# A two-block transformer on one core: GpSimd's splitting of weights by stage, the row mask on ScalarE, a restarted bank counter, and one attention branch walked backwards

## The reference

```
for l in range(2):                                  # first block
    h = rmsnorm(x) @ w_in[l]                        # 21 column groups of 128
    o = concat(sparse_attention, gated_linear_attention, spatial_gating)
    x = x + o @ w_out[l]
    h = rmsnorm(x);  x = x + (silu(h @ w_gate[l]) * (h @ w_up[l])) @ w_down[l]
x = rmsnorm(x)
h = rms_norm(x) * (1 + scl) + shift                 # second block
xa, za, q, k, v, zb, ga, gb = split(h @ w_in_2)
y_a = (lru_forward(conv(xa)) + lru_backward(conv(xa))) * silu(za) @ w_pa
y_b = neighbourhood_attention(q, k, v) * silu(zb) @ w_pb
out = rms_norm(x + gate * ((sigmoid(ga) * y_a + sigmoid(gb) * y_b) @ w_o))
```

## Time and profile before

| | us |
|---|---|
| median of 3 runs | 2053.39 |
| lowest and highest run | 2050.51 and 2055.06 |
| the profiled execution, whole | 2054.61 |
| its span, first to last instruction | 2052.6 |
| TensorE busy | 1924.2 (94%) |
| GpSimd busy | 1419.6 (69%) |
| VectorE busy | 1160.2 (57%) |
| ScalarE busy | 615.6 (30%) |
| mean granted clock of TensorE | 0.969 of full speed |

### The profile page before, as it was taken

One profiled execution on the slowest core, in us unless ns is written; L12 is line 12 of the kernel. 1 busy time (PEld: TensorE's weight loads), 2 busy tenths in 40 slices (PEclk: granted clock), 3 DMA queues, 4 the chain that ended last, 5 costly groups with the idle time before them and its releaser, 6 DMA issues.

```text
span 2052.6 us, 28491 instructions
## 1 busy us (share of the span) xinstructions
PE 1924.2 (94%) x10022; PEld 1489.2 (73%) x10022; DVE 1160.2 (57%) x1670; ACT 615.6 (30%) x1116; POOL 1419.6 (69%) x1208
## 2 busy tenths in 40 slices
PE   7898889999999999988899999997999999989997
PEld 5676557888888877755588888885777777768775
DVE  5765774466257347478556704654937666650353
ACT  4124662210011131266531100113036566540111
POOL 8554117988789985511298978886897878757772
PEclk9999989999999999999999999998999999999998
DMA  5132002343334222300124433542132233222221
GB/s 204 53 96 80 22 11 83 122 143 108 97 121 136 92 72 81 116 21 22 32 93 123 133 100 96 148 124 67 51 108 84 79 94 87 76 72 93 84 91 41
DMA packets 68680, 182.44 MB, mean 89 GB/s; under 512 B 23888, under 2 KB 24144, under 8 KB 68432
## 3 DMA queue, kind: packets, MB, share of 16 engines
q1 hardware_dynamic: 60480, 154.48, 24.8%
q10 hardware_dynamic: 8080, 26.32, 4.1%
HBM read 178.67 MB, written 2.10 MB: 88 GB/s over the span
## 4 chain that ended last, share of the span: by engine, by line
PE 70%; DVE 13%; ACT 7%; issue 6%; POOL 2%; DMA 1%; ACTq 0%; DVEq 0%; POOLq 0%
PE PS L402 21%; PE PS L406 20%; PE PS L405 20%; POOL w_lo L2083 2%; PE PS L691 1%; PE PS L653 1%; PE PS L641 1%; PE PS L441 1%; ACT P L1251 1%; ACT rg L1322 1%; DVE gN L1472 1%; DVE P L1946 1%; PE PS L538 1%; POOL w_hi L2079 1%; DVE PS L1620 1%
## 5 line engine op out<-in xcount | busy, mean ns | idle before, releaser
L2079 POOL TENSOR_TENSOR w_hi<-raw,const 128x256 fp32r<-128x256 f32 (+1 forms) x602 | 641.9, 1088 | 586.1 <-PE PS L402 578.2
L2083 POOL TENSOR_TENSOR w_lo<-raw,w_hi 128x256 fp32r<-128x256 f32 (+1 forms) x602 | 783.9, 1324 | 13.4
L402 PE MATMUL PS<-a_hi,w_hi 128*128 128x512 f32 x1616 | 651.7, 403 | 42.3 <-POOL w_lo L2083 14.1
L405 PE MATMUL PS<-a_lo,w_hi 128*128 128x512 f32 x1616 | 635.8, 393 | 0.0
L406 PE MATMUL PS<-a_hi,w_lo 128*128 128x512 f32 x1616 | 635.3, 393 | 0.0
L402 PEld LDWEIGHTS PS<-a_hi,w_hi 128*128 128x128 f32 x1616 | 307.1, 190 | 128.6 <-issue 46.0
L406 PEld LDWEIGHTS PS<-a_hi,w_lo 128*128 128x128 f32 x1616 | 307.2, 190 | 65.9
L405 PEld LDWEIGHTS PS<-a_lo,w_hi 128*128 128x128 f32 x1616 | 307.6, 190 | 64.8 <-issue 3.4
L1793 DVE TENSOR_TENSOR work<-PS,rstd 128x512 f32<-128x512 f32 x88 | 60.8, 691 | 147.6 <-PE PS L406 140.9
L402 PE MATMUL PS<-f_hi,w_hi 128*128 128x512 f32 x352 | 138.7, 394 | 0.0
L406 PE MATMUL PS<-f_hi,w_lo 128*128 128x512 f32 x352 | 138.0, 392 | 0.0
(11 more groups left out here) (290 smaller groups left out, 2494.1 us busy)
## 6 DMA issues: line engine op xcount, KB each, us to landing
raw<-weights SPq DMA_DIRECT2D x278, 512.0 KB, 3.5
work<-mod_w ACTq DMA_DIRECT2D x24, 512.0 KB, 3.6
work<-cmp_w ACTq DMA_DIRECT2D x8, 1024.0 KB, 5.6
bias<-rpb SPq DMA_DIRECT2D x256, 12.0 KB
rgw<-rgw ACTq DMA_DIRECT2D x8, 256.0 KB, 2.6
out<-xc SPq DMA_DIRECT2D x8, 256.0 KB, 2.0
const<-const SPq DMA_DIRECT2D x1, 1436.5 KB, 15.3
x<-x_t SPq DMA_DIRECT2D x4, 256.0 KB, 6.8
```

Of the source, the lines that this page charges most:

```text
L402: ins = nc.tensor.matmul(out, wh, hi, start=start, stop=False)
L405: nc.tensor.matmul(out, wh, lo, start=False, stop=False)
L2079: G.tensor_tensor(w_hi[:, r, k, :], raw[:, r, k, :], ones[:, k, :], ALU.mult).then_inc(pool_chain, 1)
L2083: ins = G.tensor_tensor(w_lo[:, r, k, :], raw[:, r, k, :], w_hi[:, r, k, :].bitcast(F32), ALU.subtract)
```

## The change

Four edits.

1. GpSimd's pieces are chosen for each slot by `parts_of`, as (w_hi pieces, w_lo pieces). (2, 2), halves of 512 columns: the first slot, the eight xa slots, and all slots of the second block from the merging gates on, 49 slots. (2, 4), w_hi in halves and w_lo in quarters: the slots of the layers' first gemms, the first two of each output product, and q, k, v, zb, za of the second block, 85 slots. (1, 1), whole: 144 slots. Before, 108 slots were in quarters and 170 whole. After every piece but the slot's last GpSimd waits for the piece's own semaphore, and w_lo of a half follows its w_hi at once. In (2, 4) the w_hi half is a tensor_scalar by 1.0 instead of a tensor_tensor with ones. The loops are gone.
2. The row mask is an activation on ScalarE behind the sigmoid, no longer a VectorE operation.
3. `aux_bank` starts at 0 again in each layer. Layer 0 does so already.
4. In attention, branch 1 takes its row blocks 3, 2, 1, 0 while branch 0 takes them 0, 1, 2, 3. And ScalarE's copy of a head pair's output stands directly behind the exponentials of unit u + 2, ahead of the compressed exponentials and the Gelus.

```diff
+def row_block(u):
+    i = u // 2 % NT
+    return i if u % 2 == 0 else NT - 1 - i
...
             for l in range(DEPTH):
-                pool_of["banks"] = 4
+                pool_of["banks"], pool_of["next"] = 4, 0
...
                         A(gN[:, :, :], PS[...], ACT.Sigmoid)\
+                            .then_inc(act_chain.sem, 1)
+                        act.wait_ge(act_chain.sem, act_chain.raised())
+                        if l == 0:
+                            act.wait_ge(const_in, 16)
+                        A(gN[:, 0, 2:24:3], gN[:, 0, 2:24:3], ACT.Copy, scale=c_("rowok"))\
                             .then_inc(emptied((l, name, "T")), 1)
...
                     if u + 2 < U:
                         exps(u + 2)
+                    if u % 8 == 0 and u:
+                        t = u // 8 - 1
+                        act.wait_ge(*filling((l, "O", t)))
+                        A(proj[:, t, :], PS[:, 6, :], ACT.Copy).then_inc(emptied((l, "O", t)), 1)
+                        act.wait_ge(*emptying((l, "O", t)))
                     if u % (2 * NT) == 0 and u + 2 * NT < U:
                         compressed_exps(u // (2 * NT) + 1)
...
-                    if u % 8 == 0 and u:
...
-                        g = gN[:, 0, 2:24:3]
-                        TS(g, g, c_("rowok"), None, ALU.mult).then_inc(dve_chain.sem, 1)
-                        dve.wait_ge(dve_chain.sem, dve_chain.raised())
...
+            def split(n, hi_parts, lo_parts):
+                r = n % RING
+                pool.wait_ge(raw_in[r], 16 * (n // RING + 1))
+                if n >= RING:
+                    pool.wait_ge(slot_used, n - RING + 1)
+                each, per = 8 // hi_parts, lo_parts // hi_parts
+                for h in range(hi_parts):
+                    k = slice(h * each, (h + 1) * each)
+                    if hi_parts == lo_parts:
+                        G.tensor_tensor(w_hi[:, r, k, :], raw[:, r, k, :], ones[:, k, :], ALU.mult).then_inc(pool_chain, 1)
+                    else:
+                        G.tensor_scalar(w_hi[:, r, k, :], raw[:, r, k, :], 1.0, None, ALU.mult).then_inc(pool_chain, 1)
+                    pool.wait_ge(pool_chain, counted())
+                    for q in range(h * per, (h + 1) * per):
+                        k = slice(q * 8 // lo_parts, (q + 1) * 8 // lo_parts)
+                        ins = G.tensor_tensor(w_lo[:, r, k, :], raw[:, r, k, :], w_hi[:, r, k, :].bitcast(F32), ALU.subtract)
+                        if q < lo_parts - 1:
+                            ins.then_inc(pool_chain, 1)
+                            pool.wait_ge(pool_chain, counted())
+                ins.then_inc(split_done, 1)
+
+            def parts_of(n):
+                kind, m = PLAN[n][0], PLAN[n][-1]
+                if n == 0 or kind in ("pa", "pb", "wo") or kind == "in2" and not KT <= m < 6 * KT:
+                    return 2, 2
+                if kind in ("in", "in2") or kind == "out" and m < 2:
+                    return 2, 4
+                return 1, 1
```

More of the change, by code:

```diff
@@ L692, in values @@
                                                    work[:, 4 + 2 * br + hh, n * P:(n + 1) * P],
-                                                   start=False, stop=br == 1 and i == NT - 1 and n == i)
+                                                   start=False, stop=u % (2 * NT) == 2 * NT - 1 and n == i)
                     if u % (2 * NT) == 2 * NT - 1:
@@ L1139, in _ @@
                 for u in range(U):
-                    i, par = u % NT, u % 2
-                    w = (u // 2 % NT + 1) * P
+                    par = u % 2
+                    w = (row_block(u) + 1) * P
                     if u >= 2:
@@ L2067, in _ @@
             G = nc.gpsimd
+            spent = [0]
             ones = c_("ones")[:, 0:1].unsqueeze(2).to_broadcast([P, 8, P])
[L2071 to L2075, removed]
-                each = 8 // pieces
-                for n in range(pieces):
-                    k = slice(n * each, (n + 1) * each)
-                    G.tensor_tensor(w_hi[:, r, k, :], raw[:, r, k, :], ones[:, k, :], ALU.mult).then_inc(pool_chain, 1)
-                for n in range(pieces):
-                    k = slice(n * each, (n + 1) * each)
-                    pool.wait_ge(pool_chain, chain + n + 1)
-                    ins = G.tensor_tensor(w_lo[:, r, k, :], raw[:, r, k, :], w_hi[:, r, k, :].bitcast(F32), ALU.subtract)
-                ins.then_inc(split_done, 1)
@@ L2086, in pieces_of, with counted @@
-            def pieces_of(turn):
-                return PIECES if any(beside_vector(item) for item in PLAN[turn * RING:(turn + 1) * RING]) else 1
-            pool.wait_ge(head_in, 16)
-            turns = SLOTS // RING
-            first, chain = 0, 0
-            while first <= turns:
-                n = pieces_of(first)
-                last = first + 1
-                while 1 <= first and last < turns and pieces_of(last) == n:
-                    last += 1
-                if 1 <= first < turns and last - first > 1:
-                    with pool.Fori(first, last) as i:
-                        for r in range(RING):
-                            split(r, i * 16 + 16, i * RING + (r - RING + 1),
-                                  i * (RING * n) + (chain + (r - RING * first) * n), n)
-                    chain += (last - first) * RING * n
-                else:
-                    last = first + 1
-                    for r in range(RING if first < turns else SLOTS % RING):
-                        split(r, 16 * (first + 1), first * RING + r - RING + 1 if first else None, chain, n)
-                        chain += n
-                first = last
+            def counted():
+                spent[0] += 1
+                return spent[0]
@@ L2112, in _ @@
+            def parts_of(n):
[5 more added lines that the diff above has]
+                return 1, 1
+            pool.wait_ge(head_in, 16)
+            for n in range(SLOTS):
+                split(n, *parts_of(n))
         @block.sync
```

14 lines of the change are left out of this document (4 added, 10 removed).

## The result

| us | before | after |
|---|---|---|
| median, lowest, highest of 4 runs | 2053.93 (2050.51 to 2055.06) | 2032.72 (2030.36 to 2032.76) |
| span of the profiled execution | 2052.6 | 2029.9 |
| its whole time | 2054.61 | 2032.75 |
| mean granted clock | 0.969 | 0.976 |

The ratio is 0.9897 with a 95% interval of 0.9879 to 0.9914: 21 us less, where 9 were forecast. The time is that of rival A, 2033, though not quite for its reason.

A forecast was written before the change was run, and what follows sets the result against it. It took the kernel as bound by TensorE, busy 94% of 2052.6 us. Its terms summed to -8.8 us against a median of 2053.4, giving 2044.5 us, with an 8-in-10 range of 2027 to 2056.

The forecast's parts named there:

- rival A: Convolution stage doesn't slow because VectorE gets in at GpSimd's pauses: about 2033 us, chance 0.30.
- start: Before the first gate gemm is through, VectorE's two-input operations wait behind w_hi halves: +1.2 us.
- Halves where it split quarters (convolution stage): Convolution stage: VectorE operations slow behind halves, so the v gemm starts late and the clock drops: +10.4 us.
- Row mask: Layer 0's decay chain: moving the mask to ScalarE ends TensorE's 7.5 us wait and its low clock: -9.2 us.
- rival D: Another VectorE operation in the same chain is shut out, so the row-mask gain doesn't come: 2053 us, chance 0.10.
- Bank counter: Start of layer 1: the restarted counter ends TensorE's 5.1 us wait for bank 0 and its low clock: -6.1 us.
- Output copy: Attention, both layers: ScalarE's earlier copy shortens TensorE's waits, only partly on the path: -5 us.
- reversal: Attention with reversed row blocks: VectorE's sum per head pair is unchanged, so no gain: 0 us.
- Halves from the gates on: Second block from the gates on: halves instead of whole slots halve TensorE's waits on two low halves: -2.3 us.
- First MLP slots: Each layer's second norm: VectorE operations meet whole pieces instead of quarters, about half of it slack: +2.2 us.
- C: GpSimd's tensor_scalar half is slow, near 2.0 us, deciding from about 1.8 us: 2070 us, chance 0.12.

The follow-up runs named there:

- e6: Changed kernel with a tensor_tensor by ones in place of the tensor_scalar for the w_hi halves of the (2, 4) slots, pauses kept: 2045.47 us, ratio 0.9969.
- e10: Changed kernel with tensor_tensor for every w_hi piece and GpSimd's old unbroken order, new piece sizes kept: 2045.45 us, ratio 0.9961.
- e1: Kernel before with only the row mask moved to ScalarE and the bank counter restarted: 2045.51 us, ratio 0.9964.
- e11: Changed kernel with the row mask back on VectorE, all else kept: 2031.54 us, ratio 0.9901.
- e12: Kernel before with only GpSimd's new pieces: 2047.36 us, ratio 0.9971.
- e8: Changed kernel with each layer's last output slot and first four MLP slots in halves, (2, 2), instead of whole: 2022.39 us, ratio 0.9845.
- e14: Changed kernel with old tensor_tensor quarters in the (2, 4) slots, all w_hi then all w_lo, a pause after each piece: 2034.29 us, ratio 0.9902.
- e5: Changed kernel with the same pieces but all w_hi first, then w_lo, so GpSimd runs without pauses: 2033.77 us, ratio 0.9901.
- e9: Changed kernel with the first MLP slots halved as in e8, and the eight xa slots in (2, 4) too: 2025.38 us, ratio 0.9872.
- e4: Changed kernel with GpSimd's old splitting (quarters or whole, no pauses, no tensor_scalar), all other edits kept: 2037.96 us, ratio 0.9923.
- e13: Changed kernel with old tensor_tensor quarters in the (2, 4) slots, all w_hi then all w_lo, no pauses, no loop: 2040.76 us, ratio 0.9929.
- e7: Changed kernel with alternating w_hi and w_lo quarters, all tensor_tensor, a pause after each, in the (2, 4) slots: 2036.84 us, ratio 0.9905.

## Why the prediction was wrong

The direction and several places were right, and the 21 us measured are well over the 9 forecast. The sum fell short because the splitting was given the wrong sign. The parts by their own runs: mask and bank -8.1, copy -4.7, reversal -3.3, pieces -5.3, together -21.4 against -21.2 measured. So they add up, as far as runs that scatter by 5 to 10 us can say it. The forecast had the pieces at +11.5 (its terms for halves, convolution, first MLP slots and start), and the mask, bank and attention at -20.3.

**The step that failed: "Halves where it split quarters (convolution stage)", +10.4.** Measured: 2.7 lost up to the v gemm, and 3.6 won right behind it. It priced 24 operations behind tensor_tensor halves at 1.57 us. Behind such halves they took 1.50, so that price was right. But GpSimd works up to four slots ahead, so only the first two of the eight rounds stood beside the xa slots. The other six stood beside (2, 4) slots. Of the tensor_scalar there I had bounded GpSimd's own duration, not what it does to VectorE. It takes 1.49 us by itself (at 1486.88), 43% more than the 1.04 of the tensor_tensor (at 1889.22), and VectorE's two-input operations go on beside it at 0.98. With that, VectorE was 5.0 later, which cost one wait of 2.9 us with its lower clock, 4.7 in all; the two waits for GpSimd went and paid part of it back. So the place and the sign of the term were right for this stage, and its size about four times too large. The first neighbourhood attention then gave more back than that: two VectorE operations (L1946, L1961) had each lasted over 5 us there before, which I had not read. With tensor_tensor halves, which is what the term assumed, the wait was 5.4 us (e6) and 8.1 (e10), so the assumption that the tensor_scalar is priced like the tensor_tensor is what failed, with the count of rounds. e6 puts it at 13 us by the medians.

**Row mask, -9.2.** The place won 11.4, and yet the step was wrong: the mask alone ends nothing (e1), and without moving it the same is won (e11). This is the forecast's other failed step: it gave the gain to the mask, and to the splitting a cost of 1.3 us here. The earlier trace rows showed a victim, and I took it for the cause. The cause was GpSimd's unbroken row of quarter pieces, and rival D (another operation shut out instead) is what the mask edit alone gives. That the sum didn't suffer is luck: another edit did the work. The remark that the measured 16.55 us decides against a wait of one piece was right for this row.

**Bank counter, -6.1.** Right; 7.8. The discount for halves in the chain didn't come.

**Output copy, -5, and reversal, 0.** -4.7 and -3.3, each alone. For the reversal I held that VectorE's sum decides; the order gave something too. The trace of all edits shows +4.8 in layer 1 and only +0.8 in layer 0. The pieces alone lose 1.9 us in layer 0's attention and win 2.8 in layer 1's (e12), which is about that difference; what in them does it stays open.

**Halves from the gates on, -2.3.** 8.1 won. The durations were as said (1.5 instead of 2.1 for y_lo). The term halved two waits, which came to 2.1 (2.9 to 1.9 and 1.8 to 0.7), and left out those for L2013 (1.4 to 0) and L2031 (1.2 to 0), 4.7 in all, and the lower clock behind two of the places (granted 0.5 at 1924 and 1996 before, full now).

**First MLP slots, +2.2.** Measured 10.4 lost. The place was right and the size wrong: I counted the last four operations and gave half of their 2.2 us away as slack. But the slowed L1384 stands ahead of the last tile's eviction, and the MLP's first matmul waits for that eviction's low half. The wait was 3.1 us plus the lower clock. e8 undid most of it.

**Rivals.** A had the right time. Its mechanism (VectorE gets in at the pauses) is true for quarters (e14) and idle with the pieces used (e5). C asked whether the tensor_scalar is slow: it takes 1.58 on the mean, under its 1.8, and behind the start TensorE doesn't wait for it. e9 shows the edge: eight such slots back to back bring waits for w_lo.

What the Trainium skill says in SBUF — State Buffer, section Who interferes with whom, a full block between a two-input VectorE instruction and GpSimd, holds here for GpSimd's tensor_tensor (1.50 us behind a half) and not for its tensor_scalar (0.98). Its line-rate for one-input work on GpSimd (GPSIMD Engine Reference, section Engine selection), by which I estimated 0.43 us, doesn't hold here: 1.49 us with VectorE idle.

## What to carry to other kernels

Before an operation that waits absurdly long is moved, ask what it waits behind: if the engine that blocks it goes on, the next one takes its place. When two engines hold each other up, as VectorE and GpSimd do here, price an instruction by what it does to the neighbour as well as by its own time, since a slower one that lets the other run can win. And find which pieces stand beside which operations from the producer's lead, here four slots, not from the stage's name.

## What the hardware showed that was not expected

- The engines don't meet only at semaphores. An unbroken row of GpSimd tensor_tensor pieces of 256 columns can hold back one VectorE operation for 12.7 to 19.3 us, over 20 to 30 pieces at full speed (before, e1 to e4, e13). The same row let VectorE in at each piece in the convolution stage (1.05 us). What decides between the two I can't say; a wait on a semaphore between the pieces ended it (e14).
- GpSimd's tensor_scalar of 512 columns took 1.49 us alone and 1.5 to 1.9 beside VectorE's convolution, its tensor_tensor for w_hi 1.04 alone and 1.2 to 1.4 there.
- The times of the changed kernel stay within 2.4 us, those of the kernel before spread by up to 11, of e6 by 8 and of e7 by 12. This wasn't pursued.
